# GpSimd keeps the weights' low part only in the last three feed-forward blocks; VectorE makes it elsewhere, and GpSimd's other work goes to VectorE and ScalarE

## The reference, cut to what matters

```
x = x + 0.5 * swiglu(rmsnorm(x), ffn1_w_in[i], ffn1_w_out[i])
x = x + mixer_i(rmsnorm(x), state_i)          # i = 0: HGRN2, i = 1: S5
x = x + 0.5 * swiglu(rmsnorm(x), ffn2_w_in[i], ffn2_w_out[i])
y = rmsnorm(x)                                # after both layers

swiglu(h):  a, b = split(h @ w_in);  (silu(a) * b) @ w_out
hgrn2, per head:  S_t = diag(f_t) S_{t-1} + k_t v_t^T;   o_t = S_t^T q_t
                  out = (o * rsqrt(mean(o*o)) * gnorm * silu(g)) @ w_out
s5, per group:    s_t = lam * s_{t-1} + B u_t;   y_t = Re(C s_t) + d * u_t
                  a, gate = split(gelu(y) @ w_glu);  out = a * sigmoid(gate)
```

## Time and profile before

| | before |
|---|---|
| median of 3 runs | 2558.6 us |
| span of the profiled execution | 2558.5 us |
| TensorE matmul (PE), busy | 2370.1 us, 93% |
| TensorE weight load (PEld, beside PE) | 2321.2 us, 91% |
| VectorE (DVE) | 1001.8 us, 39% |
| GpSimd (POOL) | 782.2 us, 31% |
| ScalarE (ACT) | 664.1 us, 26% |
| GpSimd's `w_lo` (L635) | 184 instructions, 741.6 us |

### The profile page before, as it was taken

The page is one execution under the profiler, slowest core; times in us unless marked ns, Lnnn a source line. Parts: engine busy times, 40 slices in busy tenths (PEclk is TensorE's granted clock), DMA queues, the critical chain, the costliest instruction groups (busy, mean ns, idle before and its releaser), DMA issues.

```text
span 2558.5 us, 42966 instructions
## 1 busy us (share of the span) xinstructions
PE 2370.1 (93%) x17438; PEld 2321.2 (91%) x17438; DVE 1001.8 (39%) x1538; ACT 664.1 (26%) x750; POOL 782.2 (31%) x223
## 2 busy tenths in 40 slices
PE   6989999998888888999999999999982899999998
PEld 5989999888788877999999999999972899999998
DVE  5845523756665663321122322112259323211222
ACT  3222222332222212322122322122241532221223
POOL 2332333222212212333333333333320133333332
PEclk9999999999898997999999999999986899999999
DMA  4223422441113102432332322232242333223212
GB/s 121 66 61 110 129 82 62 125 112 51 51 50 84 50 17 68 124 90 74 105 102 68 97 82 74 77 96 76 72 136 66 88 82 83 82 70 94 82 58 78
DMA packets 398491, 211.04 MB, mean 82 GB/s; under 512 B 23025, under 2 KB 393922, under 8 KB 398402
## 3 DMA queue, kind: packets, MB, share of 16 engines
q1 hardware_dynamic: 387666, 198.03, 27.9%
q10 hardware_dynamic: 10736, 11.77, 1.4%
HBM read 193.01 MB, written 20.94 MB: 84 GB/s over the span
## 4 chain that ended last, share of the span: by engine, by line
PE 57%; DVE 2%; issue 1%; ACT 1%; POOL 0%; DMA 0%; SPq 0%; DVEq 0%; ACTq 0%
PE ps L1672 55%; PE ps L1642 1%; PE ps L1971 0%; PE ps L1972 0%; DVE sq L1558 0%; DVE sq L1555 0%; DVE ssq L1556 0%; PE ps L1945 0%; POOL w_lo L635 0%; DMA wc<-wc_d 0%; DVE z_lo L1592 0%; DVE s_s L1559 0%; PE ps L1655 0%; DVE s_e L1559 0%; SPq L514 0%
## 5 line engine op out<-in xcount | busy, mean ns | idle before, releaser
L635 POOL TENSOR_TENSOR w_lo<-w_raw,w_hi 128x2048 fp32r<-128x2048 f32 (+3 forms) x184 | 741.6, 4030 | 1584.3 <-ACT w_hi L732 1584.3
L1672 PE MATMUL ps<-h_hi,w_hi 128*128 128x288 f32 x3328 | 731.6, 302 | 17.9 <-DVE t_a L1086 15.6
L1672 PE MATMUL ps<-h_lo,w_hi 128*128 128x288 f32 x3328 | 720.3, 298 | 0.0
L1672 PE MATMUL ps<-h_hi,w_lo 128*128 128x288 f32 x3328 | 719.7, 298 | 0.0
L1672 PEld LDWEIGHTS ps<-h_hi,w_hi 128*128 128x128 f32 x3328 | 544.0, 192 | 23.6 <-DVE t_a L1086 12.7
L1672 PEld LDWEIGHTS ps<-h_lo,w_hi 128*128 128x128 f32 x3328 | 544.1, 191 | 0.0
L1672 PEld LDWEIGHTS ps<-h_hi,w_lo 128*128 128x128 f32 x3328 | 543.7, 191 | 0.0
L732 ACT ACTIVATE w_hi<-w_raw 128x2048 fp32r<-128x2048 f32 (+3 forms) x184 | 309.5, 1682 | 216.5 <-PE ps L1672 204.2
L1672 PE MATMUL ps<-g_hi,w_hi 128*128 128x288 f32 x1408 | 304.7, 298 | 1.4 <-POOL w_lo L635 1.4
L1672 PE MATMUL ps<-g_lo,w_hi 128*128 128x288 f32 x1408 | 302.9, 297 | 0.0
L1672 PE MATMUL ps<-g_hi,w_lo 128*128 128x288 f32 x1408 | 302.7, 297 | 0.0
(11 more groups left out here) (301 smaller groups left out, 1975.3 us busy)
## 6 DMA issues: line engine op xcount, KB each, us to landing
w_raw<-in_ffn_w_in_dram SPq DMA_DIRECT2D x176, 512.0 KB, 4.9
w_raw<-in_ffn_w_out_dram SPq DMA_DIRECT2D x64, 384.0 KB, 3.7
w_raw<-in_ffn_w_out_dram SPq DMA_DIRECT2D x64, 320.0 KB, 3.4
w_raw<-in_hgrn_w_in_dram SPq DMA_DIRECT2D x32, 512.0 KB, 5.3
w_raw<-in_s_w_glu_dram SPq DMA_DIRECT2D x16, 512.0 KB, 4.7
wb_d<-wb_st ACTq DMA_DIRECT2D x8, 512.0 KB, 2.8
wc_d<-c_pow ACTq DMA_DIRECT2D x8, 512.0 KB, 3.5
s_in<-in_state_hgrn_dram SPq DMA_DIRECT2D x8, 512.0 KB, 4.0
```

The costliest lines, as they stand in the source:

```text
L635: nc.gpsimd.tensor_tensor(w_lo[j][:, 0:n], w_raw[j][:, 0:n], f32(w_hi[j][:, 0:n]), ALU.subtract)\
L1672: ins = M.matmul(ps[:, 2 * s + h, 0:HALF], w[j][:, at:at + P], v[:, k, h * HALF:(h + 1) * HALF], start=k == 0 and n == 0, stop=k == ph.kt ...
```

## The change

A phase is "spread" if it is an up or down phase outside ffn1_0, so ffn2_0, ffn1_1 and ffn2_1. GpSimd's queue keeps `rest` for spread phases alone. In all other phases VectorE runs `rest`:

- twice while x is loaded, ahead of the third and the sixth further tile of x;
- in up, down and glu units at the head of each unit (`rest_next`): unit j = 0 makes tile 1 of its own pair, unit j = 1 tile 0 of the next pair, before the unit waits for its PSUM tile or makes `b_part`;
- in a head, tile 1 between levels 1 and 2, tile 0 of the next head ahead of level 7.

ScalarE makes `v_seq` and `s_out` in 8 copies each with a scale per partition, ahead of `k_tok`. VectorE makes the sampled S5 states behind each half of the scan. GpSimd's constants are unchanged. VectorE's loops have their first or last units written out, and `make_masks` waits for all of GpSimd's constants (8 counts for 5).

```
+        def spread(ph):
+            return ph.kind in ("up", "down") and ph.name[0] != "ffn1_0"

 # GpSimd: rest, states and sampled_states go; what stays is
+            for ph in PH:
+                if spread(ph):
+                    with pool.Fori(0, ph.pairs) as i:
+                        for j in range(2):
+                            pool.wait_ge(w_hi_done[j], i + (ph.pair0 + 1))
+                            n = ph.size
+                            nc.gpsimd.tensor_tensor(w_lo[j][:, 0:n], w_raw[j][:, 0:n], f32(w_hi[j][:, 0:n]), ALU.subtract)\
+                                .then_inc(w_ready[j], 1)

 # ScalarE, HGRN2
+                def own_values(m):
+                    act.wait_ge(vtok_done, m + 1)
+                    if not isinstance(m, int) or m:
+                        act.wait_ge(kvs_full, m)
+                    for s in range(DEC_BATCH):
+                        ins = nc.scalar.activation(v_seq[:, s, :], v_tok[0:SAMPLE, CHUNKS, :], ACT.Copy,
+                                                   scale=own_seq[:, s:s + 1])
+                    ins.then_inc(vseq_done, 1)
+                def decayed(m, b, turn):
+                    act.wait_ge(s_ld[b], turn * 16 + 16)
+                    act.wait_ge(s_st[b], turn * 32 + 1)
+                    act.wait_ge(qk_done, m * LEVELS + SAMPLE_LEVELS)
+                    for s in range(DEC_BATCH):
+                        at = 432 + PROMPT_BLOCKS + s
+                        ins = nc.scalar.activation(s_out[b][:, s, :], s_in[b][:, s, :], ACT.Copy, scale=e_t[:, at:at + 1])
+                    ins.then_inc(decay_done, 1)
...
                     if m is not None:
+                        own_values(m)
+                        decayed(m, 1 - b, turn)
                         take_turned(m, kt_full, k_tok, ktok_done)

 # VectorE
+            def rest(ph, j, i):
+                if spread(ph):
+                    return
+                dve.wait_ge(w_hi_done[j], i + (ph.pair0 + 1))
+                n = ph.size
+                V.tensor_tensor(w_lo[j][:, 0:n], w_raw[j][:, 0:n], f32(w_hi[j][:, 0:n]), ALU.subtract)\
+                    .then_inc(w_ready[j], 1)
+            def rest_next(n, ph, j, i, last):
+                if j == 0:
+                    if not (isinstance(i, int) and i == 0) or ph.kind != "hgrn_out" and n:
+                        rest(ph, 1, i)
+                elif not last:
+                    rest(ph, 0, i + 1)
+                elif n + 1 < len(PH):
+                    rest(PH[n + 1], 0, 0)
...
                 if m:
                     norm_tile(0, m - 1)
+                if m == 3:
+                    rest(PH[0], 0, 0)
+                if m == 6:
+                    rest(PH[0], 1, 0)
...
-                dve.wait_ge(consts, 5)
+                dve.wait_ge(consts, 8)
...                                          # up units, and glu units likewise
+                    rest_next(n, ph, j, i, last)
                     dve.wait_ge(full[0], t + 1)
...                                          # down units
+                    rest_next(n, ph, j, i, last)
                     if pieces and j == 0:
                         b_part(i + ph.name[1] * (NK // 2))
                         c_part(i + ph.name[1] * (NK // 2))
...                                          # heads
                     invert(before, 0)
+                    if n is not None:
+                        rest(ph, 1, n)
+                    elif m is not None:
+                        rest(PH[n_ph + 1], 1, 0)
                     if m is not None:
                         level(m, mb, 2)
...
                         take(v_t[:], 0, n, 1)
+                        if last:
+                            rest(PH[n_ph + 1], 0, 0)
+                        else:
+                            rest(ph, 0, n + 1)
                     if m is not None:
                         level(m, mb, 7)
...                                          # S5: GpSimd's sampled_states, now on VectorE
                 scan(0)
+                sampled_states(0)
                 scan(1)
+                sampled_states(1)
```

More of the change, by code:

```diff
@@ L629, in _ @@
                                     pattern=[[DEC_SEQ, DEC_BATCH]], channel_multiplier=-1).then_inc(consts, 1)
[L631 to L679, removed]
-                        for j in range(2):
[L681 to L703, removed]
@@ L1336, in ffn_up, with down @@
                     first = 4
-                with dve.Fori(first, ph.pairs) as i:
+                with dve.Fori(first, ph.pairs - 1) as i:
                     for j in range(2):
                         unit(i, j)
-            def down(ph):
+                for j in range(2):
+                    unit(ph.pairs - 1, j, last=True)
+            def down(n, ph):
                 r = MAKES.get((ph.kind, ph.name))
@@ L1367, in down @@
                     link.n = 0
-                with dve.Fori(int(pieces), ph.pairs) as i:
+                if not pieces:
+                    for j in range(2):
+                        unit(0, j)
+                with dve.Fori(1, ph.pairs - 1) as i:
                     link.base = i * per + at
@@ L1373, in down, with hgrn @@
                     link.n = 0
+                link.base = (ph.pairs - 1) * per + at
+                for j in range(2):
+                    unit(ph.pairs - 1, j, last=True)
+                assert link.n == per
+                link.n = 0
                 link.base = at + ph.pairs * per
-            def hgrn(ph):
+            def hgrn(n_ph, ph):
                 reciprocal(1)
@@ L1536, in hgrn, with s5 @@
                 step(None, 0, None, None, HEADS - 1)
-            def s5(ph):
+            def s5(n, ph):
                 reciprocal(4)
@@ L1585, in scan, with sampled_states @@
                     dve.wait_ge(scan_done, half + 1)
+                def sampled_states(half):
+                    tiles = slice(half * half_st, (half + 1) * half_st)
+                    shape = [P, 2, DEC_BATCH, half_st]
+                    t1, t2 = (t[:, 0:ST * DEC_BATCH].rearrange("p (r b s) -> p r b s", r=2, b=DEC_BATCH) for t in z_t)
+                    before = s5_s[:, :, tiles, PROMPT_BLOCKS:].rearrange("p r s b -> p r b s")
+                    adds = s5_v[:, :, tiles, PROMPT_BLOCKS:].rearrange("p r s b -> p r b s")
+                    by = [lam8[:, q, :, tiles].unsqueeze(2).to_broadcast(shape) for q in range(2)]
+                    dve.wait_ge(sin_done, 1)
+                    first = link.begin(V.tensor_tensor(t1, before, by[0], ALU.mult))
+                    link.begin(V.tensor_tensor(t2[:, ::-1], before, by[1], ALU.mult))
+                    dve.wait_ge(dve_link, first)
+                    link(V.tensor_tensor(t1, t1, adds, ALU.add))
+                    V.tensor_tensor(s5_fs[:, :, :, tiles], t1, t2, ALU.add).then_inc(fs_done, 1)
+                    dve.wait_ge(fs_done, half + 1)
                 scan(0)
+                sampled_states(0)
                 scan(1)
+                sampled_states(1)
                 def z_rest(ct):
@@ L1617, in unit @@
                     norm_tile(5, m)
-                with dve.Fori(0, ph.pairs) as i:
+                for j in range(2):
+                    unit(0, j)
+                with dve.Fori(1, ph.pairs - 1) as i:
                     for j in range(2):
                         unit(i, j)
-            for ph in PH:
-                {"up": ffn_up, "down": down, "hgrn_in": hgrn, "hgrn_out": down, "glu": s5}[ph.kind](ph)
+                for j in range(2):
+                    unit(ph.pairs - 1, j, last=True)
+            for n, ph in enumerate(PH):
+                {"up": ffn_up, "down": down, "hgrn_in": hgrn, "hgrn_out": down, "glu": s5}[ph.kind](n, ph)
             dve.wait_ge(rms_root, 1)
```

38 lines of the change are left out of this document (21 added, 17 removed).

## The result

The changed kernel takes 2484.96 us (median of 4 runs, 2482.88 to 2486.41) where the kernel before takes 2558.56: a ratio of 0.9711, 95% interval [0.9697, 0.9725]. The profiled spans are 2484.7 and 2558.5 us. Every sign was right; the mixer gave half as much again as was counted.

A forecast was written before the change was run, and what follows sets the result against it. The prediction took VectorE's stalls behind GpSimd, with TensorE's waits and half clock, to bound the unsaturated stretches: HGRN -46.0, first 155 us -9.7, down blocks +10.7, S5 +0.4, together -44.6 from 2558.5, told as 2514 us; range 2495 to 2534.

The forecast's parts named there:

- the mixer: HGRN stage: stalls and half clock gone, less the added waits, -46.0 us in all.
- The half clock: HGRN heads: the half clock behind the long e_t gap goes, 2.1 us in each of seven places, 15 us.
- rival (C): Heads and down blocks: the clock holds better than counted, 11 and 4 us less, total 2499; chance 0.10.
- The added waits in the heads: HGRN heads: VectorE's two added w_lo cost 1.65 us in six heads, 0.3 and 0.8 in the others, 11 us.
- the wait at the start of the output projection: hgrn_out: the first refill of w_lo gets 1.1 us shorter, 1.22 for 2.36.
- Rival A: Heads: VectorE's additions lie fully on the level chain, 4.6 instead of 1.65 us a head, total 2540; chance 0.10.
- The stall itself: HGRN heads: of TensorE's waits, 32.9 of 35.0 us for e_t and all 9.3 for q_t go, 42.2 together.
- rival B: Levels: the stalls aren't GpSimd's, so nothing goes and VectorE's additions cost, total about 2620; chance 0.04.
- The down blocks: ffn1_0's two down blocks: rest, waiting for w_hi, holds b_part up in VectorE's queue, +10.7 us.
- The first 155 us: Start of the run, x loading and first units: shorter VectorE stalls and t_a waits, less half clock, -9.7 us.
- S5: S5 scan: 4.5 us of stalls go, the sampled states on VectorE add 4.8, +0.4 with link waits.
- ScalarE's copies: HGRN heads: ScalarE's 16 copies, 4.2 us each for v_seq and s_out, fit in idle time before k_tok, cost 0.

The follow-up runs named there:

- e2: Changed kernel with VectorE's w_lo between levels 1 and 2 of each head made three times: 2545.11 us, ratio 0.9938.
- e12: Kernel of e2 with 18 extra identity matmuls on TensorE filling the gap ahead of its wait for the next level: 2526.20 us, ratio 0.987.
- e11: Changed kernel with all four GpSimd instructions of a head back (w_lo twice, v_seq, s_out): 2551.07 us, ratio 0.9971.
- e6: Changed kernel with the w_lo of each pair's second tile behind b_part instead of ahead, in ffn1_0's two down blocks: 2464.88 us, ratio 0.9631.
- e10: Changed kernel with GpSimd making w_lo again in the first up block of ffn1_0: 2496.99 us, ratio 0.9762.
- e1: Changed kernel with VectorE's w_lo between levels 1 and 2 of each head made twice: 2509.40 us, ratio 0.9809.
- e3: Changed kernel with VectorE's w_lo ahead of level 7 made twice: 2503.80 us, ratio 0.9781.
- e4: Changed kernel with only the heads' w_lo back on GpSimd; v_seq and s_out stay on ScalarE: 2531.66 us, ratio 0.989.
- e5: Changed kernel with only v_seq and s_out back on GpSimd; w_lo stays on VectorE: 2499.29 us, ratio 0.9765.

## Why the prediction was wrong in size

*The half clock* was counted at too few places. The sum had "2.1 in each of seven places: 15", all of them behind a wait for `e_t`, and nothing for the rest of the stage; busy time fell by 27.4. Behind those waits the price was about right: from the level behind the gap to the end of the head TensorE is busy 2.3 us longer in the mean than in the kernel after in five of the six whole heads, 0.1 in the sixth (its gap was 2.58 us) and 1.7 in the head ahead of them, 13.1 in all. The other 14.3 us stood in the sum at nothing: 7.3 in the six heads ahead of the gap (about 1.6 each in three heads that have the half clock behind `sq`, and 0.4 in every head, at the full clock), 3.1 in the stretch ahead of them, which has a wait of 2.50 us for `q_t` with the half clock behind it, and 3.8 in the last head and behind it. One head of before, ahead of the gap and from it on, and then the same of the kernel after (a few records are missing; columns as in the earlier trace rows):

```profile
817.20:857.21 40.01, 34.20 (x234) 31.25 (x233) 24.41 (x36) 10.20 (x12) 12.78 (x4) 0.94 0.30 80
857.21:871.14 13.93, 13.93 (x89) 13.76 (x89) 9.53 (x21) 2.72 (x4) 0.00 (x0) 0.80 0.00 0
```

```profile
674.52:707.57 33.05, 32.25 (x235) 29.77 (x234) 19.56 (x39) 13.07 (x22) 0.00 (x0) 1.00 0.35 98
707.57:718.84 11.27, 11.27 (x92) 11.10 (x90) 10.42 (x20) 4.55 (x12) 0.00 (x0) 1.00 0.00 0
```

Of all this I had only named the heads' start, in a rival (C) of 11 us at 0.10. The row that had the whole of it was there: a stage clock of 0.91 in the earlier trace rows is 0.09 of 458, about 41 us, and some 12 of it are left after the change. e2 and e12 show that TensorE's gap brings the half clock behind it. Why it is gone behind `sq` as well stays open: e11, with GpSimd's instructions back, has it there in three of the six heads, but e6 and e10, without them, have it in two each. The clock is the larger part of what the mixer's sum missed, 12.4 of 22.4 us.

*The added waits in the heads* were the other: "1.65 in six heads ... 11" measured next to nothing: 1.9 for `e_t` where 2.1 was to be left, and 2.3 for `w_lo` where 1.3 stood in the sum. Idle time, without the wait at the start of the output projection, went down by 40.2, for 29.9 counted (42.2 - 11 - 1.3): 10.3. I counted 1.6 us of room for VectorE at the first place (2.28 - 0.65) and 1.3 at the second; it has 2.45 at either (2.22 + 0.23 and 2.28 + 0.17). e1 and e3 show that the room ends there: another copy costs 2.0 us of waiting a head and slower work besides. Rival A, the same term at its worst, fell with it. The wait at the start of the output projection got 0.9 shorter, for 1.1 counted.

*The stall itself* was right: 32.9 of 35.0 and 9.3 were to go, and 33.1 and 9.3 went. That it is GpSimd's (rival B fell) e4, e5 and e11 show.

*The down blocks* cost 6.2 for the 10.7 counted. The mechanism was right and shows in the row of 225.41: a pair takes 249.94 - 225.41 = 24.5 us where 24.8 was counted. The size was not, as the waits of before in this stretch show beside the 20.9 above:

```profile
PE ps L1642 <- DVE b_pow L1260: 15.6, 8, 4.7
PE ps L1672 <- POOL w_lo L635: 1.4, 2, 0.8
```

The waits for `b_pow` grew by 5.3, not by some 10, GpSimd's 1.4 went, and 2.3 more of busy time (356.44 for 354.11) came with the clock: 6.2. The rule that it leaned on is borne out: the Trainium skill (TensorE: Matmul & The Clock Gate, § Architectural detail: the array is 16× 32×32, not 1× 128×128) has VectorE take its instructions strictly in order, and e6 is the measurement, 20.1 us for moving one waiting instruction behind a ready one.

*The first 155 us* gave 11.8 for 9.7, the last wait for `t_a` falling to 5.0 as said. *S5* came out at +0.5 for +0.4, in part by luck. In the kernel after the first half of the scan with its sampled states runs from 1833.54 to 1871.57, 38.0 us, and the second takes 35.8 without them: 4.4 went and twice 2.1 came. Both together end 75.96 us after their start, for 76.07 before, which is -0.1; the rest of the +0.5 lies behind the scan.

ScalarE's copies cost nothing, as said. Groups by form of ScalarE in one head of the kernel after:

```profile
L836 ACT ACTIVATE s_out<-s_in,e_t 128x128 f32<-128x128 f32 x8 | 2.4, 392 | 0.0
...
L816 ACT ACTIVATE k_tok<-ps 128x512 f32<-128x512 f32 x1 | 0.6, 599 | 5.0 <-PE ps L1672 5.0
```

`s_out` and `v_seq` are busy 2.4 us each (4.2 together were counted; one lasts 0.39 us for 0.26, but they overlap), and ScalarE still stands 5.0 us ahead of `k_tok`, where 10 had been left by the count.

## What to carry to other kernels

A wait of TensorE costs its length and often a slower clock behind it, and the same stage can have the slow clock at other places too; price it from the clock of the whole stage (what the granted clock lacks of 1, times the length, or the busy time of the same instructions in two traces), not from the instructions that stand right behind the gap. A helper's instruction on a busy engine was free here up to the room that the engine had at that place and paid in full or more beyond it, so measure the room as the distance from the result to its reader. And on an engine that works in order, put what is ready ahead of what has to wait: that was worth 20 us here, more than a quarter of the change.

## What the runs showed of the hardware that I had not expected

With a gap of 2.0 us in each of six heads, e1's heads have a mean clock of 0.95 and 14.1 us more of busy time than the kernel after, though only three of the gaps have the half clock right behind them. The clock also falls without such a gap: in e6 two heads took 47.1 and 45.8 us, with the half clock behind `sq` and no wait above 0.8, as in the other heads of 44.3. It didn't make e6's mixer longer. The 2676 instructions take 390.5 us there for 393.0 in the kernel after, because the clock is higher at their end: 0.94 over the last 267 instructions, for 0.79.

Which instructions of VectorE GpSimd holds up can be read from the least, middle and longest duration of two lines of the kernel before (ns), one with an operand in PSUM, one with both in SBUF.

```profile
L1086 DVE TENSOR_TENSOR t_a<-ps,rstd x88: 756/758/759, 47.3 to 2473.7; 128x576 f32<-128x576 f32 x88
...
L1401 DVE TENSOR_TENSOR q_t<-q_t,e_t x48: 421/438/6614, 570.8 to 954.5; 128x256 f32<-128x256 f32 x32, 128x288 f32<-128x288 f32 x16
```

The first is never held, though GpSimd is busy 304.24 of the 840 us in which half of its instructions lie; the second is held up to 6.6 us. The Trainium skill (SBUF — State Buffer, § Who interferes with whom) says that a VectorE instruction with two inputs in SBUF contends with a GpSimd instruction that reads SBUF, that one with at most one such input, outside its two-port modes, doesn't, and that the shared ports are an exclusive lock; the two rows agree. One row more shows that a waiting VectorE isn't let in between two GpSimd instructions that follow one another: the `q_t` of 743.45 in the earlier trace rows, 6.61 us long, outlasts the rest of this `s_out` and the whole of the `w_lo` behind it (GpSimd, kernel before).

```profile
743.43 1.89 POOL L650 TENSOR_TENSOR s_out<-s_in,e_t 128x1024 f32<-128x1024 f32 x1
```
